# Expert weights in panels of 1,792 features: longer runs per transfer, a narrow expert second, and the last gate's first token tile straight in fp32

## What is computed

```python
D_MODEL, SEQ, D_FF, N_EXPERTS, TOP_K = 1024, 256, 3584, 8, 2
def swiglu(x, w_gate, w_up, w_down):
    return (jax.nn.silu(x @ w_gate) * (x @ w_up)) @ w_down
def moe_swiglu(x, w_router, w_gate, w_up, w_down):
    logits = (x @ w_router).astype(jnp.float32)
    top_vals, top_idx = lax.top_k(logits, TOP_K)
    weights = jax.nn.softmax(top_vals, axis=-1)
    ...
    for e in range(N_EXPERTS):
        out = out + combine[..., e:e + 1] * swiglu(x, w_gate[e], w_up[e], w_down[e])
# end of layer 1
h = layer_norm(ALPHA * h + f, ln_g[i, 1], ln_b[i, 1])
h = h + jax.nn.sigmoid(h @ ple_w_gate[i] + ple_b_gate[i]) * (p[i] @ ple_w_proj[i])
```

## Time and profile before

| | us |
|---|---|
| median of 3 runs | 1474.23 |
| lowest, highest | 1471.96, 1474.25 |
| the profiled execution | 1470.26 |
| its span, first to last instruction | 1468.5 |
| PE busy in it | 1412.5 |
| DVE, ACT busy in it | 702.5, 319.8 |
| granted TensorE clock, mean | 0.993 |

### The profile page before, as it was taken

How to read it: one execution, slowest core, us unless ns; L and a number is a source line. 1 busy time by engine, 2 the same in 40 slices (tenths; PEclk the granted TensorE clock), 3 DMA queues, 4 the chain that set the end, 5 groups by cost and what they waited for, 6 DMA issues and landing times.

```text
span 1468.5 us, 27721 instructions
## 1 busy us (share of the span) xinstructions
PE 1412.5 (96%) x12131; PEld 925.5 (63%) x12131; DVE 702.5 (48%) x1128; ACT 319.8 (22%) x432; POOL 24.6 (2%) x51
## 2 busy tenths in 40 slices
PE   8999999999999999999999999999999999999687
PEld 7888788888778877356666664456454454465135
DVE  4795678878874668432332332241422322323247
ACT  4444344344455553000000000000000000000012
POOL 3010000000000000000000000000000000000100
PEclk9999999999999999999999999999999999999998
DMA  9956445555456126999999999999999999999980
GB/s 367 337 197 248 165 172 183 189 200 185 166 177 207 50 78 262 419 412 404 416 414 419 420 419 420 419 418 421 419 419 420 419 420 419 420 420 415 417 348 30
DMA packets 135481, 467.99 MB, mean 319 GB/s; under 512 B 8524, under 2 KB 9376, under 8 KB 134848
## 3 DMA queue, kind: packets, MB, share of 16 engines
q1 hardware_dynamic: 130864, 450.92, 77.9%
q0 software_dynamic: 2992, 12.70, 2.3%
q10 hardware_dynamic: 1504, 2.62, 0.5%
HBM read 462.53 MB, written 3.67 MB: 317 GB/s over the span
## 4 chain that ended last, share of the span: by engine, by line
PE 78%; DMA 13%; DVE 5%; ACT 2%; issue 1%; SPq 1%; POOL 0%; ACTq 0%; POOLq 0%; DVEq 0%
PE ps L1781 76%; DMA ring<-in_moe_w_up_dram 10%; DMA ring<-in_moe_w_down_dram 2%; DMA raw<-in_ple_w_gate_dram 1%; DVE split L1121 1%; PE ps L1799 1%; ACT split L751 1%; DVE h L1169 1%; DVE stats L1173 1%; DVE acc L1164 1%; DVE htl L1136 0%; SPq L578 0%; PE ps L2116 0%; PE ps L2152 0%; DVE acc L1216 0%
## 5 line engine op out<-in xcount | busy, mean ns | idle before, releaser
L1781 PE MATMUL ps<-ring,xt 128*32 128x448 f32 x5632 | 546.2, 542 | 25.9 <-DMA ring<-in_moe_w_up_dram 25.6
L1781 PEld LDWEIGHTS ps<-ring,xt 128*32 128x32 f32 x5632 | 256.7, 110 | 300.0 <-issue 242.1
L1781 PE MATMUL ps<-split,hth 128*128 128x512 f32 x1168 | 366.7, 395 | 6.0 <-DVE htl L1136 2.8
L1699 DVE TENSOR_TENSOR m_hb<-ps,m_sg 128x224 f32<-128x224 f32 x88 | 29.2, 385 | 575.8 <-ACT m_sg L1054 575.8
L1781 PE MATMUL ps<-ring,m_bt 128*32 128x256 f32 (+1 forms) x3472 | 278.4, 469 | 6.8 <-DMA ring<-in_moe_w_down_dram 6.7
L1781 PEld LDWEIGHTS ps<-split,hth 128*128 128x128 f32 x1168 | 218.9, 190 | 53.8 <-DVE htl L1136 3.4
L1781 PEld LDWEIGHTS ps<-ring,m_bt 128*32 128x32 f32 x3472 | 173.0, 110 | 108.7 <-issue 28.8
L1781 PE MATMUL ps<-split,htl 128*128 128x512 f32 x584 | 229.3, 393 | 0.0
L1707 DVE STREAM_TRANSPOSE m_bt<-m_hb 32x224 f32<-32x224 f32 x352 | 205.1, 583 | 5.5
L1054 ACT ACTIVATE m_sg<-ps 128x224 f32<-128x224 f32 x88 | 25.4, 357 | 727.7 <-PE ps L1781 727.7
L1121 DVE TENSOR_TENSOR split<-raw,split 128x2048 fp32r<-128x2048 f32 x52 | 118.7, 2291 | 64.0 <-ACT split L751 63.9
(11 more groups left out here) (256 smaller groups left out, 651.1 us busy)
## 6 DMA issues: line engine op xcount, KB each, us to landing
ring<-in_moe_w_gate_dram SPq DMA_DIRECT2D x128, 896.0 KB, 17.2
ring<-in_moe_w_up_dram SPq DMA_DIRECT2D x128, 896.0 KB, 16.6
ring<-in_moe_w_down_dram SPq DMA_DIRECT2D x128, 896.0 KB, 16.2
raw<-in_gm_w_in_dram SPq DMA_DIRECT2D x14, 1024.0 KB, 14.6
raw<-in_ffn_w_gate_dram SPq DMA_DIRECT2D x14, 1024.0 KB, 5.0
raw<-in_ffn_w_up_dram SPq DMA_DIRECT2D x14, 1024.0 KB, 5.0
raw<-in_ffn_w_down_dram SPq DMA_DIRECT2D x14, 1024.0 KB, 5.0
raw<-in_fox_w_in_dram SPq DMA_DIRECT2D x12, 1024.0 KB, 4.9
```

The lines of the kernel that those rows point to most:

```text
L1699: ins = nc.vector.tensor_tensor(m_hb[:, q, :], ps[bank][:, QTR:2 * QTR], m_sg[:, q, :], ALU.mult)
L1781: return nc.tensor.matmul(o, a, b, start=start, stop=stop)
```

## The change

- `PANEL` is 1,792, so there are 16 blocks of 24 slots. A slot of gate or up weights is now one chunk of 128 rows by 1,792 columns, in runs of 7,168 bytes. PE computes all gate products of a block, then all up products, each in a matmul of 448 columns, and gives slots back one by one. The slots keep their size.
- Down weights come in four transfers of two slots each, in runs of 14,336 bytes, with semaphores of their own (`down_landed`).
- A narrow block stands second in `ORDER`, another seventh; the two blocks of the emptiest expert stand last.
- The gather is made in two halves: that for the first four experts in use before the first block, the other between `gate_up(1)` and `down(0)` (`HALF_1`).
- `xh` and `xl` move to other memory and are made earlier on ACT and DVE, and the last ring slots wait for the router's logits (`lg_full`) in place of the gather. The first 16 slots are filled in the order `FILL`.
- `m_bt` has one buffer (and one more for the last block), and the product of silu and up is written over `m_sg`. `gate_up(b)` waits for the hidden values of block b - 1 (`e_hid`), the silu for its transposes.
- In the last gate, tile 0 is transposed as fp32 into `ht` and multiplied in fp32 with the unsplit weights in `raw`; tile 1 uses the split weights as before. The load of the activation table for the square root stands ahead of the last copy.

```diff
-PANEL = 896
+PANEL = 1792
...
-    SLOT = 2 * PANEL
-    X_BLK = 12
+    SLOT = PANEL
+    X_BLK = 24
...
+        order = [(e, j) for e in range(BIG) for j in range(NPAN)]
+        order.insert(1, (BIG, 0))
+        order.insert(6, (BIG, 1))
+        return order + [(NE - 1, j) for j in range(NPAN)]
...
+        def expert_cols(w, e, j, k):
+
+            part = w[0, 0:1] if e == 0 else w[0, bass.ds(expert_of[e], 1)]
+            return part[:, k * P:(k + 1) * P, j * PANEL:(j + 1) * PANEL].rearrange("e p n -> p e n")
...
-            return part[:, :, i * SLOT:(i + 1) * SLOT]
+            return part[:, :, i * 2 * SLOT:(i + 1) * 2 * SLOT]
...
-                sp.wait_ge(gx_full, 2 * KD)
+                sp.wait_ge(lg_full, T)
...
             def hidden(b):
-                if r is not None or b:
-                    dve.wait_ge(bt_ready, hid0 + b)
-                banks = hid_banks(r, b)
+
+                dve.wait_ge(s0["used"], used0 + (G_MOE + gu_at(b) + 2 * KD))
+                banks = up_banks(b)
...
             def turn_hidden(b):
+
                 dve.wait_ge(e_hid, hid0 + (b + 1))
+                if 0 < b < NB - 1:
+                    dve.wait_ge(s0["used"], used0 + (G_MOE + down_at(b - 1) + 8))
...
             for b in range(NB + 1):
                 if b < NB:
                     if b == 0:
+                        gather(0, at_e, gx0)
+                        pe.wait_ge(gx_act, gx0 + KD // 2)
+                        pe.wait_ge(gx_dve, gx0 + KD // 2)
+                    else:
+                        pe.wait_ge(e_hid, hid0 + b)
+                    gate_up(b)
+                    if b == HALF_1:
+                        pe.wait_ge(route_ready, 1)
+                        gather(1, at_e, gx0)
+                        pe.wait_ge(gx_act, gx0 + KD)
+                        pe.wait_ge(gx_dve, gx0 + KD)
...
+        def last_ple():
+
+            st = streams[1]
+            for nb in range(2):
+                bank = ps[GATE_BANKS[nb]]
+                for k in range(KD):
...
+                    last = mm(bank[:, :], ht[:, k, 0:P], raw[:, 2 * nb + k // 4, k % 4, :], k == 0, k == KD - 1)
+                last.then_inc(last_gate, 1)
+                if nb == 0:
+                    last_turn(1)
```

More of the change, by code:

```diff
@@ L95, in block_order @@
     def block_order():
[L97 to L106, removed]
+        order = [(e, j) for e in range(BIG) for j in range(NPAN)]
+        order.insert(1, (BIG, 0))
+        order.insert(6, (BIG, 1))
+        return order + [(NE - 1, j) for j in range(NPAN)]
     ORDER = block_order()
     FINISHED = [e for e, j in ORDER if j == NPAN - 1]
-    assert len(ORDER) == NE * NPAN and FINISHED[-1] == NE - 1
+    assert FEW == 2 and NPAN == 2 and len(ORDER) == NE * NPAN and FINISHED[-1] == NE - 1
     def narrow(b):
@@ L404, in build_trunk @@
     ring_landed = [sem(f"ring_landed{i}") for i in range(RING)]
+    down_landed = [sem(f"down_landed{i}") for i in range(4)]
     bt_ready = sem("bt_ready")
@@ L1055, in experts @@
                         .then_inc(e_silu, 4 - len(banks) if q == len(banks) - 1 else 1)
+                if b == HALF_1:
+                    gathered(1, gx0)
+                if b == HALF_1 and r is None:
+                    act.wait_ge(gx_full, 2 * KD)
+                    for m in range(T):
+                        nc.scalar.mul(acc[:, m, :], h[:, m, :], ALPHA).then_inc(acc_init, 1)
                 if b and ORDER[b - 1][1] == NPAN - 1:
@@ L1204, in norm @@
                     scale_bias(h, acc, m, part, par[:, 2 * n + 1, part]).then_inc(streams[which]["h"], 1)
-            for q in range(2):
-                stream_lo(q, T - 1, which)
+            if which == 0:
+                for q in range(2):
+                    stream_lo(q, T - 1, which)
         def residual(k, g_end):
@@ L1608, in _ @@
         by_place(slots[:, :, 0:NE], slots_e)
-        def first_experts(half):
-            return slice(4 * half, 4 * half + 4)
-        select_every(first_experts, (0,))
-        rest_x(0)
-        select_every(first_experts, (1,))
+        for half in range(2):
+            select_half(half, lambda e, n: slice(e, e + n))
         def route_weights():
@@ new lines, in last_turn @@
+        def last_turn(m, between=None):
+            for q in range(2):
+                if q and between is not None:
+                    between()
+                pe.wait_ge(streams[1]["h"], 2 * m + q + 1)
+                if m:
+                    pe.wait_ge(streams[1]["tp_hi"], q + 1)
+                for c in range(4):
+                    last = nc.tensor.transpose(ps[6 + q][:, c * P:(c + 1) * P],
+                                               h[:, m, (4 * q + c) * P:(4 * q + c + 1) * P], ident[:, :])
+                last.then_inc(streams[1]["tp"], 1)
```

526 lines of the change are left out of this document (268 added, 258 removed).

## The result

The changed kernel takes 1453.64 us (median of 3 runs, 1453.64 to 1453.84) against 1474.23; the ratio is 0.9866, with a 95% interval of 0.9843 to 0.9888. The three runs of the kernel before were high ones: 35 later runs of it lie between 1470.28 and 1475.67, with medians of 1471.2, 1472.0 and 1472.7. Run again beside 13 of them, the changed kernel took 1453.95 us, a ratio of 0.9882 (0.9866 to 0.9899). The two profiled executions can be taken apart row by row; by their spans the gain is 1468.5 - 1451.8 = 16.7 us. It is this number that I account for. (A second profile of the changed kernel has a span of 1452.8.)

The account below looks back on a forecast made before the run. DMA was taken to bound the mixture, by 65 us over PE. Start -2.5, pace -8.3, ring +1.0, last transfer +1.8 and tail -4.2 sum to -12.2 us: 1474.2 to 1462.0 us, range 1450 to 1474.

Parts of the forecast that it names:

- The pace: Mixture's weight transfers: longer runs make all of them 1.0% quicker over 830.6 us, -8.3 us.
- My lower bound: Pace of transfers: longer runs give nothing, since 2,048-byte runs at 28 to 42 us also moved 419 GB/s.
- The start: Before the mixture: half the gather precedes the list of experts, so SP's next transfer comes at 587.2; -2.5 us.
- The ring: Early mixture: new wait for block 0's hidden values and the gather's second half cause a short SP stall; +1 us.
- The single `m_bt`: Wide blocks: twelve transposes take 14.0 us, covered by 18.04 us of gate products; costs nothing.
- The last transfer: End of the mixture: it is two slots, so PE begins four rows of panels instead of two; +1.8 us.
- The tail: Last gate after the down stage: earlier PE start and no standing between tiles, against longer fp32 products; -4.2 us.
- The sentence on the table load: Tail: the 1.28 us load between last variance and its root moves ahead, under the last down products.
- 1.8% or more: Rival on the mixture's pace: longer runs gain 1.8%, 1456.3 us, or 2.5%, 1452; chance 0.20.
- Nothing: Rival on the mixture's pace: longer runs bring nothing, leaving -3.9 us, 1470.3; chance 0.22.
- slower addresses: Rival on the mixture's transfers: the new address pattern slows them, +19 us at 2.3%, 1489; chance 0.09.
- PE behind: Rival early in the mixture: second half-gather and new wait cost 12 us more, 6 reach SP, 1468; chance 0.07.

Follow-up runs that it names:

- the transfers alone: Kernel with only SP's queue streaming expert weights, nothing computed; mixed as in a block, long runs move 423 GB/s, short runs 411.
- The kernel with the early list: Changed kernel, but DVE writes the list of experts ahead of the copies of the gather's first half; 1453.43 us.
- the kernel with pairs: Changed kernel with its own runs of 7,168 bytes, but PE waits for gate and up slots in pairs and frees them in pairs; 1453.44 us.
- the kernel with the narrow block third: Changed kernel with its first narrow block third in the order instead of second; 1463.12 us.
- The kernel with the filler: Kernel before the change, with 40 instead of 4 small PE products between tile 0's last transposes and its first gate product; 1470.78 us.
- either order of the casts: Changed kernel without the early activation, 1453.13 us; the same with ACT's first two last-gate casts ahead of the first root, 1452.67 us.
- the kernels that have the short runs back: Changed kernel with gate and up runs of 3,584 bytes, 1462.21 us; down runs of 7,168, 1455.90 us; both, 1465.33 us.

## Why the prediction was right, step by step

The forecast of 1462.0 had the sign and the three sources right; the time, 1453.6, lies 8.4 us lower, inside the range of 1450 to 1474, but below the 1458 to 1466 that was called likeliest.

- **Where that difference comes from.** 4.5 us are in the spans: 12.2 forecast, 16.7 measured. The rest is that the forecast was counted from the median of 1474.2, while the later medians of that kernel are 1471.2 to 1472.7. From the profiled execution, 1470.3, the same sum gives 1458.1.
- **The pace, mis-sized.** Forecast 1.0%, -8.3 us; measured -12.0, 1.4%. The cause is shown: run length alone gives 11.6 us. My lower bound, nothing, rested on the 28 to 42 us window and read it wrongly, since half of its bytes came through POOL's queue. The upper bound, 1.8%, from two pairs of rows, was nearer. The 1.0% was a choice between the two, no reading. The rule of the Trainium skill, "DMA: Bandwidth & Descriptors", section "Why small descriptors are slow (HBM only)", a fixed overhead for every packet, is what all runs show in kind; the 1.1% worked out from it, an estimate, is under the 1.4% of the kernel and under the 2.9% of the transfers alone (423 against 411).
- **The start, wrong.** Forecast -2.5, measured -0.5. The gather started at 576.10 (575.9 forecast) but took 7.6 us instead of 5.7: the granted clock was 0.50 from 574 to 580 (windows below). Why it fell isn't shown: a pause of 2.0 us stood ahead of the fall, but one of 2.1 us in the kernel before left the clock at 1.00. A second step failed too: "SP's next transfer at 587.2" was taken to move the mixture with it. The kernel with the early list had it at 587.22, and won nothing. The end goes with PE's first product, which was forecast at 582.3 and came at 584.42.
- **The ring, right in place.** The wait for the hidden values was 1.80 us (2.2 forecast), the second half of the gather 6.5 us (8.1), and SP ran short around 620 and 692 us: against 422 GB/s, the 20 us at 393 and the 10 at 397 are 2.0 us. The kernel before had as much below its own rate, three of the 36.7-us slices of its page (412, 404 and 416 where 419 is usual, 2.2 us), so that in the difference the term of +1.0 came out at about nothing. That was luck, for it isn't the same loss: the share there was 1.01 to 1.03, the engines were busy, and why they moved less isn't shown. Nor is the place fixed: the kernel with pairs moved 422 GB/s from 620 to 640 us, and instead 351, 398 and 412 from 590 to 620, and ended as early. That the early lead is small is shown by the kernel with the narrow block third, 10 us slower.
- **The single `m_bt`, right.** Twelve transposes took 11.57 us of the 14.0 allowed (at 773.98), and PE's timeline shows no wait for them.
- **The last transfer, right**: 3.64 us against 1.92, +1.7 (+1.8 forecast).
- **The tail, right in place, 1.7 short.** Forecast -4.2, measured -5.9. PE's start, forecast 2.9 earlier against the down stage, came 3.1 earlier. The fp32 products took 13.4 us (13.8), those of tile 1 11.5 (10.9). The 1.7 us of lost clock that I left in did not come. The kernel with the filler shows why: the fall follows PE's pause, and the changed kernel has none. The sentence on the table load had the right sum from the wrong edit: the early activation is worth nothing, and the load stays hidden with either order of the casts, now that the weights are there in time.
- **The rivals.** "1.8% or more" came near in time (1456.3) but not in its reason; the other part of that is the tail. "Nothing" falls with the kernels that have the short runs back, "slower addresses" with the equal 420 GB/s. "PE behind" did not occur, but the narrow block third shows its price.

## What to carry to other kernels

Where the DMA engines are busy all the time, count the runs: here each cost 0.23 to 0.28 ns in the kernel, 0.6 ns alone, so that 89,000 packets in place of 131,000 gave 11.6 us of 1,470 at the same bytes. Around a ring that is filled at the start, ask which of the two ends gives back the first slots: here an issue 1.94 us earlier won nothing, the end went with the first product, and the order of the first three blocks was worth 10 us. And before a clock loss or a table load is counted, look at what ends last behind it: in the kernel before, the lost clock of tile 0 lay under another wait.

## What was not expected of the hardware

- The cost of a run is about twice as high on a queue alone as in the kernels: 423 against 411 GB/s alone, 425 against 419 in the kernels, with the same mix. Why is open.
- Runs of 1,792 bytes move 381 GB/s and runs of 14,336 move 428, over the same 16 engines at a DMA share of 1.06 and 1.01: the share doesn't tell how well the engines are used.
- The clock fell in front of the gather. Windows of the changed kernel:

```profile
572.00:574.00 2.00, 1.69 (x25) 1.49 (x25) 1.67 (x9) 0.00 (x0) 0.00 (x0) 0.81 1.00 419
574.00:576.00 2.00, 0.07 (x1) 0.00 (x0) 1.90 (x10) 0.00 (x0) 0.00 (x0) 0.50 1.02 430
576.00:578.00 2.00, 1.90 (x6) 1.94 (x7) 1.02 (x4) 0.25 (x1) 0.00 (x0) 0.50 1.01 423
578.00:580.00 2.00, 2.00 (x8) 2.00 (x7) 0.56 (x1) 0.23 (x1) 0.00 (x0) 0.50 1.04 431
```

  PE stood still from 570.33 to 572.32 and again from 574.08 to 576.10, with small products between. From 572 to 574 the clock is 0.81 in the mean and 0.50 thereafter, so about the last 0.8 us of these two were already at 0.50: the fall came behind the first pause and ahead of the second. The same stretch of the kernel before, behind its pause of 2.09 us:

```profile
572.00:574.00 2.00, 1.38 (x8) 1.42 (x9) 2.00 (x3) 0.00 (x0) 0.00 (x0) 1.00 1.02 418
```

  The half gather took 7.6 us in place of 5.7, so the fall costs about 2 us of PE's start and, if the end goes with that start, as much of the whole, an estimate. To keep PE busy in the pauses was not tried.
